# The normed tokens' two parts stored in channel order, and the gather's stationary loads reading them with a step of eight

## The reference

```python
h = rmsnorm(x, norm2_gain[l])
x = x + moe_ffn(h, router_w, router_b, w_gate[l], w_up[l], w_down[l])
...
# moe_ffn: a router picks 2 of 16 experts for a token (both from one group of four), weights them, and adds
ys = (silu(xb @ w_gate[e]) * (xb @ w_up[e])) @ w_down[e]
```

## Time and profile before

| | |
|---|---|
| median of 3 runs | 1199.56 us (1198.37 to 1200.16) |
| profiled execution | 1196.86 us, span 1195.1 us |
| busy in it | PE 1120.1 us (94%), PEld 815.0 us, DVE 585.6 us, ACT 475.3 us |
| moved by DMA | 312.93 MB, 262 GB/s on the mean |
| mean granted clock of TensorE | 0.977 |

### The profile page before, as it was taken

The page is one execution under the profiler, slowest core; times in us unless marked ns, Lnnn a source line. Parts: engine busy times, 40 slices in busy tenths (PEclk is TensorE's granted clock), DMA queues, the critical chain, the costliest instruction groups (busy, mean ns, idle before and its releaser), DMA issues.

```text
span 1195.1 us, 17180 instructions
## 1 busy us (share of the span) xinstructions
PE 1120.1 (94%) x6564; PEld 815.0 (68%) x6564; DVE 585.6 (49%) x931; ACT 475.3 (40%) x741; POOL 0.2 (0%) x4
## 2 busy tenths in 40 slices
PE   5999999999996999999879999999999879999997
PEld 4997888999974344333369978889999754443433
DVE  5658584556555133312256495745666533322222
ACT  4667566565541011101156764655555401110100
POOL 0000000000000000000000000000000000000000
PEclk9999999999997999999989998999999979999999
DMA  8553353253576999999934543452345869999995
GB/s 325 194 175 131 126 203 142 79 204 141 209 279 287 418 378 429 429 429 427 407 139 165 188 142 138 145 188 93 143 177 199 321 286 405 405 428 428 428 428 217
DMA packets 62626, 312.93 MB, mean 262 GB/s; under 512 B 3024, under 2 KB 3152, under 8 KB 50256
## 3 DMA queue, kind: packets, MB, share of 16 engines
q1 hardware_dynamic: 62544, 311.85, 66.2%
HBM read 310.79 MB, written 1.05 MB: 261 GB/s over the span
## 4 chain that ended last, share of the span: by engine, by line
PE 77%; DMA 11%; DVE 6%; issue 3%; ACT 2%; DVEq 0%; SPq 0%; ACTq 0%
PE slot L558 24%; PE slot L574 15%; PE M L852 12%; PE slot L883 9%; DMA ring_down<-in_w_down 9%; PE slot L761 3%; PE slot L814 2%; DMA ring_up<-in_w_up 2%; PE slot L533 1%; PE M L736 1%; PE M L714 1%; DVE w_lo L1237 1%; PE slot L830 1%; PE M L685 1%; PE M L662 1%
## 5 line engine op out<-in xcount | busy, mean ns | idle before, releaser
L1237 DVE TENSOR_TENSOR w_lo<-ring,w_hi 128x1024 fp32r<-128x1024 f32 x200 | 240.5, 1222 | 153.0 <-ACT w_hi L928 151.9
L928 ACT ACTIVATE w_hi<-ring 128x1024 fp32r<-128x1024 f32 x200 | 208.4, 1053 | 128.1 <-PE slot L574 59.4
L558 PE MATMUL slot<-hT_hi,w_hi 128*128 128x256 f32 x640 | 183.9, 287 | 0.0
L558 PE MATMUL slot<-hT_hi,w_lo 128*128 128x256 f32 x640 | 181.0, 283 | 0.0
L558 PE MATMUL slot<-hT_lo,w_hi 128*128 128x256 f32 x640 | 181.0, 283 | 0.0
L883 PE MATMUL slot<-ring_down,arena 128*64 128x512 f32 x512 | 123.2, 610 | 13.2 <-DMA ring_down<-in_w_down 9.8
L574 PE MATMUL slot<-w_hi,hT_hi 128*128 128x512 f32 x320 | 129.2, 404 | 3.3 <-DVE w_lo L1237 3.3
L574 PE MATMUL slot<-w_lo,hT_hi 128*128 128x512 f32 x320 | 125.9, 394 | 0.0
L574 PE MATMUL slot<-w_hi,hT_lo 128*128 128x512 f32 x320 | 125.8, 393 | 0.0
L558 PEld LDWEIGHTS slot<-hT_hi,w_hi 128*128 128x128 f32 x640 | 122.7, 192 | 1.1 <-DVE w_lo L1237 0.8
L558 PEld LDWEIGHTS slot<-hT_lo,w_hi 128*128 128x128 f32 x640 | 122.7, 192 | 0.3
(11 more groups left out here) (257 smaller groups left out, 1660.3 us busy)
## 6 DMA issues: line engine op xcount, KB each, us to landing
ring<-in_w_in SPq DMA_DIRECT2D x40, 2048.0 KB, 7.9
ring_down<-in_w_down SPq DMA_DIRECT2D x32, 2048.0 KB, 15.7
ring<-in_w_gate SPq DMA_DIRECT2D x16, 2048.0 KB, 14.5
ring_up<-in_w_up SPq DMA_DIRECT2D x16, 2048.0 KB, 17.1
arena<-in_w_gate SPq DMA_DIRECT2D x16, 2048.0 KB, 21.5
ring<-in_w_up SPq DMA_DIRECT2D x8, 2048.0 KB, 17.7
ring_odd<-in_w_up SPq DMA_DIRECT2D x8, 2048.0 KB, 26.5
ring<-in_w_branch SPq DMA_DIRECT2D x6, 2048.0 KB, 8.0
```

What stands on the lines that cost most here:

```text
L558: last = mm(o[:, (n * tiles + m) * T:(n * tiles + m + 1) * T], w[:, cc, m * P:(m + 1) * P], h[:, cc, :], start=cc == k == 0, stop=cc == ro ...
L928: A(piece_of(w_hi, i), source(i), ACT.Copy).then_inc(hi_ready.sem, 1)
L1237: v.tensor_tensor(piece_of(w_lo, i), source(i), piece_of(w_hi, i), ALU.subtract)\
```

## The change

Both parts are written as they lie in xs, with no step in any operand. The gather's stationary operand takes the 128 channels 8p + c out of the 1024 of a token, one in eight. Its values, the products and their number are as before. The change moves no instruction on any engine: each engine's program has the same instructions in the same order, and only the access patterns of three of them differ. After it the numbers of the lines below L1138 are lower by one, and those below L1482 by three.

```diff
--- before.py
+++ after.py
@@ -811,7 +811,7 @@
                         o = G0[:, bank * 512 + c2 * 256:bank * 512 + (c2 + 1) * 256]
                         for t in range(NT):
                             for k, part in enumerate((hn_hi, hn_lo)):
-                                last = mm(o, part[:, t, cc * P:(cc + 1) * P], sel[:, t, :],
+                                last = mm(o, part[:, t, :].rearrange("q (p c) -> q c p", c=DC)[:, cc, :], sel[:, t, :],
                                           start=t == k == 0, stop=t == NT - 1 and k == 1)
                     last.then_inc(xg_ps, 1)
 
@@ -1135,8 +1135,7 @@
                     norm_stats(1, t)
                 for t in range(NT):
                     act.wait_ge(diag_ready.sem, diag_ready.at(l, NT + t + 1))
-                    A(hn_hi[:, t, :].rearrange("q (c p) -> q c p", c=DC),
-                      xs[:, t, :].rearrange("q (p c) -> q c p", c=DC), ACT.Copy, scale=rinv[:, t:t + 1]).then_inc(hn_hi_ready.sem, 1)
+                    A(hn_hi[:, t, :], xs[:, t, :], ACT.Copy, scale=rinv[:, t:t + 1]).then_inc(hn_hi_ready.sem, 1)
                 act.wait_ge(rt_max.sem, rt_max.at(l, 1))
                 A(rt(2), rt(1), ACT.Exp).then_inc(rt_exp.sem, 1)
 
@@ -1479,10 +1478,8 @@
                     take_hT(1, t, g2[:, 0, :])
                 for t in range(NT):
                     dve.wait_ge(hn_hi_ready.sem, hn_hi_ready.at(l, t + 1))
-                    v.scalar_tensor_tensor(out=hn_lo[:, t, :].rearrange("q (c p) -> q c p", c=DC),
-                                           in0=xs[:, t, :].rearrange("q (p c) -> q c p", c=DC),
-                                           scalar=rinv[:, t:t + 1],
-                                           in1=hn_hi[:, t, :].rearrange("q (c p) -> q c p", c=DC), op0=ALU.mult, op1=ALU.subtract)\
+                    v.scalar_tensor_tensor(out=hn_lo[:, t, :], in0=xs[:, t, :],
+                                           scalar=rinv[:, t:t + 1], in1=hn_hi[:, t, :], op0=ALU.mult, op1=ALU.subtract)\
                         .then_inc(hn_lo_ready.sem, 1)
```

## The result

The changed kernel takes 1203.07 us (median of 7 runs, 1202.5 to 1204.06), the kernel before 1198.37 us (7 runs beside them, 1196.07 to 1200.47). The ratio is 1.0039 with a 95% interval of 1.0029 to 1.0049: slower by 4.7 us, 3.5 to 5.9 by the interval. The forecast was 4.0 us more, and 1204.0 us.

The account below looks back on a forecast made before the run. It took serial waits around hn_lo and the router, then the weights' DMA queue, as the bound. -3.0 + 1.1 + 2.1 + 2 x 1.9 = +4.0 us on 1199.56, rounded up to 1204.0 us; range 1196.0 to 1208.5.

Parts of the forecast that it names:

- The 1.54 us ahead of the router: Before the router's first operation: shorter hn_lo gains at most 1.54 us, taken as 1.5 us per layer, 3.0 in two.
- The load isn't hidden: Gather on TensorE: load and product take the same time, so whatever a load gets longer is added to the spacing.
- Its price: Gather load with a step of eight: 0.12 us more, so 0.235 us at full clock, 0.24 at half clock.
- a free load: Rival, gather loads: the step costs TensorE nothing, only the 3.0 us gain remains, 1196.5 us; chance 0.25.
- a load that doubles in clock cycles: Rival, gather loads: doubled at half clock too (0.43 us), +7.8 us in sum, 1207.4 us; chance 0.12.
- 48 exposed, 80 covered: Gather loads per layer: 48 count in the time, the other 80, 9.3 us, are hidden by the DMA backlog.
- First quads: First four experts' gather in each layer, on the path: 7.7 us, +1.1 in layer 0 and +2.1 in layer 1.
- half of the second: First 16 loads of the second four experts' gather, ahead of the slot-freeing down product: +1.9 us in each layer.
- 8.5 us of backlog: DMA queue after 430.39: work until 464.7, so the next down at 456.20 may come 8.5 us late without loss.
- The level: Whole kernel: base of 1199.56 us plus 4.0, rounded up for half-clock unknowns to 1204.0 us.

Follow-up runs that it names:

- the storing half: Kernel before with only hn_hi and hn_lo written in channel order, gather loads side by side as before: 1194.62 us against 1197.96, ratio 0.9971.
- the pair order: Kernel before with neighbouring channels stored in pairs, hn_lo in four instructions a tile, gather loads at a step of two: 1197.05 us, ratio 0.9990.
- The second quad alone: Kernel before with channel order stored and only each layer's second four experts' gather loaded with a step of eight: ratio 1.0018.
- the version with the moved pieces: Kernel before with channels stored in pairs, loads at a step of two, three of eight hn_lo pieces moved to VectorE's wait for ranks: 1194.88 us against 1197.81.
- third and fourth quad: Kernel before with channel order stored and only each layer's last 64 of 128 gather loads at a step of eight: ratio 0.9976.
- both versions with moved work: Paired channels with three hn_lo pieces moved, ratio 0.9973; kernel before with only its second hn_lo moved to VectorE's wait for ranks, ratio 0.9997.

## Why the prediction was right

**The 1.54 us ahead of the router.** Read from two rows, VectorE's end of hn_lo and TensorE's end of the logits: 1.54 and 1.56 us a layer came back. That it fits to the hundredth is luck. I took hn_lo to shrink by 1.66 us and the logits to cap the gain at 1.54. hn_lo takes 1276 ns, not 1224, and shrank by 1.55 us; that is the whole gain, and the logits, ready 0.05 us before it, capped nothing. The two were near enough for either reading to give the same time.

**The load isn't hidden.** That the gather's load and product take the same time was the step from which the rest follows, and it held: the load's record gained 0.147 us, the spacing at full clock 0.123.

**Its price.** I took 0.235 us at full clock and 0.24 at the lower level; both are 0.24. This was the bold step, since the rows of two other engines had to stand for TensorE's, and a free load (0.25) and a load that doubles in clock cycles (0.12) would have fitted the same trace of before. What carried it was that ScalarE and VectorE, whose own paces differ, both came to about 1.9 ns an element: 128 x 1.9 = 0.24 us. In that there is some luck: the 150 ns taken off for a fixed part stand in no row. Measured on the very operations, the step adds (2145 - 1133) / 1024 = 0.99 ns an element on ScalarE and (2055 - 1276) / 1024 = 0.76 on VectorE, 0.13 and 0.10 us for 128; the spacing gained 0.12, in between. Why TensorE has the same pace no run shows. The load's record is 0.337 us, not 0.31; for that I have no cause.

**48 exposed, 80 covered.** First quads +1.35 and +2.34 (forecast +1.1 and +2.1), half of the second +1.97 (+1.9), the last 64 loads 0.6 us by their own experiment. How they split between the layers hangs on when the clock rises: in the storing half the first quads take 6.06 and 6.13 us instead of 6.60 and 5.61, and the same 3.7 us in sum would have been +1.89 and +1.82. The margin is smaller than my text made it look, though. I worked out 8.5 us of backlog at one issue; what the two later quads use up is TensorE's own waits, and in the changed kernel none of those for down weights is left. A load with twice that price would not have been hidden, by my estimate: 160 loads would take 39 us, and the loads' waits for weights were 21.4.

**The level.** 1204.0 was built on a median of 1199.56 from three runs; seven runs have 1198.37. The difference of 4.7 us lies 0.3 us above the 4.4 that I gave after rounding. The terms as measured make -3.1 + 3.7 + 3.9 = +4.5 us, the two stages +4.0: in layer 1 they grew by 2.07 us where its terms make 2.75, and the traces don't name what took up the rest.

**Where an expectation failed** it was in the sizes of an experiment. For the pair order I put 0.34 us on a piece of 256 elements, from its length alone; it costs 0.41, and eight of them eat half of the gain. Moving three of them away gave it back. The second quad alone cost 1.7 us more by its ratio than its half quad of exposed loads; by its trace it cost no more than these, and the cause of the difference stays open.

## What to carry to other kernels

A step that is moved from one engine's operand to another's is not gone: ask for each engine whether its reader is at its limit there. Here the step cost VectorE 1.55 us a layer, and all of it counted; TensorE loads the same elements four times, and 48 of its 128 loads lie where it has no slack.

Ask how close the elements that are read one after the other lie, and not only whether there is a step. With pairs of float32 side by side ScalarE and VectorE read at nearly full pace here, and TensorE's loads took a step of two at no cost (196 against 190 ns), so a layout between the two extremes served both sides; then look for the idle place of the engine that pays for the shorter instructions.

Before counting on "hidden behind the DMA", find the last issue that still follows the engine at once. Everything ahead of it counts in full; behind it, the sum of the engine's waits is the budget.

## What was not expected of the hardware

The load with a step has the same spacing at both levels of the clock, 0.24 us, while one without has 0.206 to 0.215 us at the lower and 0.119 us at the upper. At full clock the 32 loads of a first quad would pay 3.9 us; layer 0 paid 1.35 and layer 1 2.34, as both run partly at the lower one.

The clock can also fall while TensorE works without a gap. In the version with the moved pieces, stretches of its profiled execution read:

```profile
359.00:361.00 2.00, 2.00 (x20) 2.00 (x20) 2.00 (x4) 0.61 (x1) 0.00 (x0) 0.99 1.00 426
361.00:362.00 1.00, 1.00 (x7) 1.00 (x6) 0.92 (x3) 0.00 (x0) 0.00 (x0) 0.50 1.03 442
```

TensorE had waited 1.55 us up to 356.63 and then made transposes and logits without a gap, yet it went to 0.50 at 361. The logits took 4.62 us instead of 3.64, and the router of layer 0 started only 0.6 us earlier than before; in layer 1, where it didn't happen, the gather started 1.6 us earlier. In the kernels before and after, the clock fell only behind the logits. It is not the moved pieces that do it: the same fall, in one of the two layers, is in five of the ten experiments' profiled executions (pair order, second quad, third and fourth quad, both versions with moved work), and the logits take 4.30 to 4.62 us there. The wait of 1.55 us ahead of the transposes is in the other executions as well, so what decides is open.
